# Sparse attention and last block of a three-part transformer kernel: square sums, rotations, constants, selection rounds and norm spreads placed elsewhere

## The reference, cut to what matters

```python
q, k, v, qi, ki, wi = split(h @ w_in)
q = partial_rope(rms_norm(q per head, q_g)); k = partial_rope(rms_norm(k per head, k_g))
score = sum over index heads of wi * relu(qi @ ki.T), -inf above the diagonal
idx = top_k(score, 64)                      # per query
p = softmax(q @ k[idx].T * scale); out = (p @ v[idx]) @ w_o
```

## Time and profile before

| | us |
|---|---|
| median of 3 runs | 1600.78 |
| lowest, highest | 1599.29, 1606.47 |
| the profiled execution's own time | 1597.11 |
| its span (first to last instruction) | 1595.3 |
| TensorE products busy | 1546.4 (97%) |
| VectorE, ScalarE, GpSimd busy | 660.8, 781.2, 1137.6 |
| mean granted TensorE clock | 0.988 |

### The profile page before, as it was taken

How to read it: one execution, slowest core, us unless ns; L and a number is a source line. 1 busy time by engine, 2 the same in 40 slices (tenths; PEclk the granted TensorE clock), 3 DMA queues, 4 the chain that set the end, 5 groups by cost and what they waited for, 6 DMA issues and landing times.

```text
span 1595.3 us, 40789 instructions
## 1 busy us (share of the span) xinstructions
PE 1546.4 (97%) x16162; PEld 1481.1 (93%) x16162; DVE 660.8 (41%) x1615; ACT 781.2 (49%) x1296; POOL 1137.6 (71%) x848
## 2 busy tenths in 40 slices
PE   6999999989999999999999999999999999999998
PEld 6999999878899999999999987699999987799998
DVE  4334468764446333223332257643351435442200
ACT  5444557633345444454444444654445535565532
POOL 5876757983438878778787784088878974478885
PEclk9999999999899999999999999999999999999999
DMA  7544543310023544455444541065536542235552
GB/s 268 185 166 145 178 149 133 106 68 3 2 82 110 198 168 151 164 194 195 167 150 164 188 164 51 10 241 199 183 130 204 192 139 107 80 133 184 185 185 79
DMA packets 37909, 231.31 MB, mean 145 GB/s; under 512 B 4527, under 2 KB 6680, under 8 KB 16552
## 3 DMA queue, kind: packets, MB, share of 16 engines
q1 hardware_dynamic: 36552, 228.57, 40.7%
q10 hardware_dynamic: 1248, 1.24, 0.2%
HBM read 228.67 MB, written 2.63 MB: 145 GB/s over the span
## 4 chain that ended last, share of the span: by engine, by line
PE 74%; DVE 2%; issue 1%; ACT 1%; POOL 0%; DVEq 0%; POOLq 0%; ACTq 0%
PE PS L841 59%; PE PS L840 1%; PE PS L1100 1%; PE PS L1107 1%; PE PS L1515 1%; PE PS L1115 1%; PE PS L1491 1%; PE PS L1139 1%; PE PS L1145 1%; PE PS L1501 1%; PE PS L1291 0%; PE PS L1090 0%; PE PS L1283 0%; PE PS L1679 0%; PE PS L1667 0%
## 5 line engine op out<-in xcount | busy, mean ns | idle before, releaser
L795 POOL TENSOR_TENSOR wlo<-raw,whi 128x256 fp32r<-128x256 f32 (+1 forms) x742 | 1071.1, 1476 | 362.2 <-ACT whi L2739 340.3
L841 PE MATMUL PS<-xh,whi 128*128 128x272 f32 (+1 forms) x2304 | 666.6, 289 | 21.6 <-POOL wlo L795 16.9
L841 PE MATMUL PS<-xl,whi 128*128 128x272 f32 (+1 forms) x2304 | 658.4, 286 | 0.0
L841 PE MATMUL PS<-xh,wlo 128*128 128x272 f32 (+1 forms) x2304 | 657.8, 285 | 0.0
L2739 ACT ACTIVATE whi<-raw 128x1024 fp32r<-128x1024 f32 x468 | 455.4, 982 | 359.3 <-PE PS L841 338.2
L841 PEld LDWEIGHTS PS<-xh,whi 128*128 128x128 f32 x2304 | 434.4, 189 | 31.1 <-issue 23.2
L841 PEld LDWEIGHTS PS<-xl,whi 128*128 128x128 f32 x2304 | 435.6, 189 | 0.5
L841 PEld LDWEIGHTS PS<-xh,wlo 128*128 128x128 f32 x2304 | 436.0, 189 | 0.0
L841 PE MATMUL PS<-hid_h,whi 128*128 128x272 f32 (+1 forms) x960 | 273.8, 285 | 2.1 <-POOL wlo L795 1.6
L841 PE MATMUL PS<-hid_h,wlo 128*128 128x272 f32 (+1 forms) x960 | 273.8, 285 | 0.0
L841 PE MATMUL PS<-hid_l,whi 128*128 128x272 f32 (+1 forms) x960 | 272.8, 284 | 0.0
(11 more groups left out here) (426 smaller groups left out, 1640.3 us busy)
## 6 DMA issues: line engine op xcount, KB each, us to landing
raw<-w_f_in_in SPq DMA_DIRECT2D x88, 1024.0 KB, 4.8
raw<-w_f_dn_in SPq DMA_DIRECT2D x64, 704.0 KB, 4.0
raw<-w_b_ff_in SPq DMA_DIRECT2D x32, 1024.0 KB, 4.8
raw<-w_rk_k_in SPq DMA_DIRECT2D x4, 1024.0 KB, 4.8
raw<-w_rk_r_in SPq DMA_DIRECT2D x4, 1024.0 KB, 4.8
raw<-w_rk_v_in SPq DMA_DIRECT2D x4, 1024.0 KB, 5.1
raw<-w_rk_o_in SPq DMA_DIRECT2D x4, 1024.0 KB, 5.3
raw<-w_at_q_in SPq DMA_DIRECT2D x4, 1024.0 KB, 4.9
```

The costliest lines, as they stand in the source:

```text
L795: last = nc.gpsimd.tensor_tensor(wlo[U % SPL][:, piece], raw[U % RAW][:, piece], whi[U % SPL][:, piece].bitcast(F32), ALU.subtract)
L841: mm(out, a, b, start=start and n == 0, stop=stop and n == 2, **kw)
```

## The change

In the sparse attention TensorE takes the four square sums as 0 and 1 before value tile 0, 2 and 3 before value tile 2. Rotations 1 and 2 are both issued in loop step 0, rotation 3 stays in step 4. The constants go from three groups of six (steps 3, 5, 6) to two groups of three (steps 3 and 5), with the wait of step 6 moved to step 7. On VectorE the last pair of rounds and the end of block 0's selection come before `query_cosine(2)` instead of behind it. In the last block the four pairs of spreads of part a stand two and two: two before and two in the middle of the second half of `b_values(0, .)`; the two key spreads come behind `attend(0)` and `attend(1)`, and VectorE's two key scalings at the end of its steps 1 and 2. The tile of normalised probabilities `prnb` leaves the place where it covered part of the spread table and now covers four tiles of the key's work, for which `krot` is put beside the other three. No instruction on ScalarE, GpSimd or SyncE changes.

```diff
--- before.py
+++ after.py
@@ -447,12 +447,13 @@
         craw = b2("craw", [128, 2, 2, SEQ])
         squares = Region(rings)("squares", [128, 8, SEQ])
         b2.here = rings + 4 * 8 * SEQ
+        prnb = Region(b2.here)("prnb", [128, 2, 2, SEQ])
         kr = b2("kr", [128, SEQ])
         kg = b2("kg", [128, SEQ])
         krs = b2("krs", [32, SEQ])
+        krot = b2("krot", [128, SEQ])
         lgb = Region(b2.here)("lgb", [128, 2, 2, SEQ])
         ksq = b2("ksq", [128, 4, SEQ])
-        krot = b2("krot", [128, SEQ])
         qn = b2("qn", [128, 4, SEQ])
         qr = b2("qr", [128, 2, SEQ])
         qg = b2("qg", [128, 2, SEQ])
@@ -485,8 +486,6 @@
         posf = tb("posf", [128, SEQ])
         freq = tb("freq", [128, 2])
         spread = tb("spread", [16, 1280])
-
-        prnb = Region(posi_at)("prnb", [128, 2, 2, SEQ])
         ptb = tb("ptb", [128, 2, 2, SEQ])
         assert used[0] <= nc.sbuf_usable_end, (used[0], nc.sbuf_usable_end)
 
@@ -1469,15 +1468,15 @@
             last.then_inc(s_hrot, 1)
             query_rotation(0)
             query_sum(0)
+            query_sum(1)
             U, G = U0["at_v"], G0["at_v"]
             pe.wait_ge(s_lo, 2 * U + 2)
             pe.wait_ge(s_free, G - 1)
             pe.wait_ge(s_hsq, 4)
             value_tile(0, PS[:, bank(G), 0:256])
-            query_sum(1)
             query_sum(2)
+            query_sum(3)
             value_tile(2, PS[:, bank(G), 256:512]).then_inc(s_part, 1)
-            query_sum(3)
 
             o0 = G0["at_o"]
             def head_scores(j):
@@ -1537,13 +1536,19 @@
                     head_transposes(j - 1)
                 if 0 <= j - 2 < 16:
                     head_values(j - 2)
-                if j in (1, 2, 4):
-                    if j == 4:
-                        pe.wait_ge(s_hout, 3)
-                    query_rotation({1: 1, 2: 2, 4: 3}[j])
-                if j in (3, 5, 6):
-                    pe.wait_ge(s_hout, {3: 3, 5: 4, 6: 5}[j])
-                    constants(6, PS[:, ahead + (j == 5), 0:128])
+                if j == 0:
+                    query_rotation(1)
+                    query_rotation(2)
+                if j == 3:
+                    pe.wait_ge(s_hout, 3)
+                    constants(3, PS[:, ahead, 0:128])
+                if j == 4:
+                    query_rotation(3)
+                if j == 5:
+                    pe.wait_ge(s_hout, 4)
+                    constants(3, PS[:, ahead + 1, 0:128])
+                if j == 7:
+                    pe.wait_ge(s_hout, 5)
                 if j in (7, 8):
                     output_part(0, j - 7)
                 if j in range(9, 18, 2):
@@ -1580,19 +1585,20 @@
                     if norm and mi == 0:
                         norm_sum(norm, SEQ)
 
-            def b_values(u, q):
+            def b_values(u, q, part=range(4)):
                 name = ("b_va", "b_vb")[u]
                 U, G = U0[name], G0[name]
                 pe.wait_ge(s_lo, 2 * U + q + 1)
                 if q == 0:
                     pe.wait_ge(s_free, G - 1)
-                for k in range(4 * q, 4 * q + 4):
+                for k in [4 * q + d for d in part]:
                     for j in range(2):
                         tb_ = slice(j * 128, j * 128 + 128)
                         last = products(PS[:, G % 2, j * 256:j * 256 + 256], weights(U, ALLR, slice(k * 256, k * 256 + 256)),
                                         (xh[0][:, k, tb_], xl[0][:, k, tb_]), k == 0 and j == 0, k == KC - 1, tokens=True,
                                         skip_group_check=True)
-                last.then_inc(s_unit, 1)
+                if 3 in part:
+                    last.then_inc(s_unit, 1)
 
             def b_queries(u, q):
                 U, G = U0["b_uq"] + u, G0["b_uq"] + u
@@ -1756,29 +1762,42 @@
             pe.wait_ge(s_hinv, AT2 + 1)
             pe.wait_ge(s_rcd, 2)
             pe.wait_ge(b_cc, 1)
-            for n, j in enumerate((0, 4, 2, 6)):
+            def head_spread(n):
+                j = (0, 4, 2, 6)[n]
                 for q in range(2):
                     last = mm(PS[:, 4 + n, q * SEQ:q * SEQ + SEQ], spread_two(16, j + q), hinva[:, :], start=True, stop=True)
                 last.then_inc(s_hb, 1)
-            b_values(0, 1)
-            pe.wait_ge(s_hinv, AT2 + 2)
-            for q in range(2):
-                last = mm(PS[:, 2, q * SEQ:q * SEQ + SEQ], spread_rope(q), hinvb[:, :], start=True, stop=True)
-            last.then_inc(s_hb, 1)
-            for n in range(2):
+
+            def rope_spread():
+                pe.wait_ge(s_hinv, AT2 + 2)
+                for q in range(2):
+                    last = mm(PS[:, 2, q * SEQ:q * SEQ + SEQ], spread_rope(q), hinvb[:, :], start=True, stop=True)
+                last.then_inc(s_hb, 1)
+
+            def key_spread(n):
                 if n:
                     pe.wait_ge(s_hsc, AT_HSC + 5)
                 for q in range(2):
                     last = mm(PS[:, 3 - n, q * SEQ:q * SEQ + SEQ], spread_two(8, 2 * n + q), hinvb[:, :], start=True, stop=True)
                 last.then_inc(s_hb, 1)
+
+            head_spread(0)
+            head_spread(1)
+            b_values(0, 1, range(2))
+            head_spread(2)
+            head_spread(3)
+            b_values(0, 1, range(2, 4))
+            rope_spread()
             pe.wait_ge(s_hsc, AT_HSC + 2)
             scores(0)
             pe.wait_ge(s_x, X0["cq"] + 3)
             b_queries(0, 0)
             attend(0)
+            key_spread(0)
             b_queries(0, 1)
             pe.wait_ge(s_hsc, AT_HSC + 4)
             attend(1)
+            key_spread(1)
             b_queries(1, 0)
             attend(2)
             b_queries(1, 1)
@@ -2419,9 +2438,9 @@
             top_rounds(0, 1)
             dve.wait_ge(s_hroot, 1)
             v.reciprocal(hinvk[0:4, :], hinvk[0:4, :]).then_inc(s_hinv, 1)
-            query_cosine(2)
             top_rounds(0, 1)
             top_end(0)
+            query_cosine(2)
             dve.wait_ge(s_hb, 1)
             dve.wait_ge(s_free, G0["at_k"] + 1)
             v.scalar_tensor_tensor(kT[:, :, :], kT[:, :, :], col(VEC["k_g"]), PS[:, 6:8, 0:T],
@@ -2616,7 +2635,8 @@
             dve.wait_ge(b_rotd, 1)
             v.tensor_tensor(krf[:, :, :], krot[:, :].unsqueeze(1).broadcast_to([128, 2, SEQ]), spread_pair(2),
                             ALU.mult).then_inc(s_hsc, 1)
-            for n in range(2):
+
+            def key_scale(n):
                 dve.wait_ge(s_hb, AT_HB + 6 + n)
                 x = kn[:, 2 * n:2 * n + 2, :]
                 v.scalar_tensor_tensor(x, x, gqk[:, 0:1], spread_pair(3 - n), ALU.mult, ALU.mult).then_inc(s_hsc, 1)
@@ -2686,6 +2706,8 @@
                     dve.wait_ge(s_unit, 2 * (U0["b_uq"] + 1))
                     v.tensor_scalar(qg[:, :, :], chunk_pair(G), col(VEC["qb_r"]), None, ALU.mult).then_inc(b_qg, 1)
                     queries_drain(0, qr[:, :, :])
+                if J in (1, 2):
+                    key_scale(J - 1)
                 if J == 3:
                     queries_drain(1, qn[:, 0:2, :])
                 if J == 4:
```

## The result

| | before | after |
|---|---|---|
| median of 20 runs, us | 1601.45 | 1597.95 |
| lowest, highest | 1597.60, 1612.94 | 1589.15, 1603.93 |
| profiled execution's own time, its span | 1597.11, 1595.3 | 1599.32, 1597.5 |
| its mean granted clock | 0.988 | 0.983 |

The ratio after to before is 0.9972, with a 95% interval of 0.9959 to 0.9984: 4.5 us less (2.6 to 6.6), inside the 0.5% that I call the same. The ratio is estimated over all runs of both; the two medians alone lie 3.5 us apart. The profiled execution of after is 2.2 us slower than that of before although the medians stand the other way. So the two traces can't be subtracted as wholes; they have to be read stage by stage, with the clock beside each length.

What follows compares the result with a forecast made beforehand. TensorE, with 74% of the chain, was taken as the bound. Attention -5.92 us (idle, low clock and constants won, less 3.17 of new waits) and last block +0.2 made -5.7: 1600.78 to 1595.1 us, range 1590.5 to 1599.8.

Steps and rivals of the forecast that it cites:

- (1): Sparse attention, before score products 2: TensorE waits for VectorE's logits 1, 0.53 us.
- (2): Sparse attention, before transposes 0: TensorE waits for VectorE's probabilities 0, 0.71 us.
- (3): Sparse attention, before transposes 1: TensorE waits for ScalarE's copy of transposes 0, behind half a weight copy, 0.87 us.
- (4): Sparse attention, before transposes 2: TensorE waits for ScalarE's copy 1, behind the second half weight copy, 0.76 us.
- (5): Sparse attention, before transposes 3: TensorE waits some 0.30 us, with VectorE's rotation sums 1 and 2 in its steps 2 and 3.
- With the clock full: Sparse attention, steps 0 to 6: filling the hole keeps full clock, winning about 3 us of low clock.
- Rival A: Sparse attention, thinned steps: the clock falls again for 6.8 us, 2.2 us lost, gain 3.5, 1597.3 us; chance 0.17.
- A gain is excluded, since no wait stands there to be filled: Last block, reordered spreads: no time can be won, as TensorE's only waits there lie at 1352 and later.
- the price of changing kinds: Last block: one more change from full products to spreads and back costs 0.2 us, bounds 0 and 0.4.
- B: Sparse attention: ScalarE's and VectorE's strings close up, no new waits, 9.1 us less there, 1591.9 us; chance 0.09.
- D: Sparse attention, steps 1 to 5: VectorE is the bound and the constants were cover, gain 2.6, 1598.2 us; chance 0.10.
- C: Sparse attention: the constants held the clock; without them low clock persists, 1606.6 us with the last block; chance 0.04.

Runs made afterwards that it cites:

- again: The changed kernel unaltered, measured a second time against the kernel before: median 1595.83 us, ratio 0.9958.
- attention_only: The change's attention edits alone, with the last block of the kernel before: 1600.89 us, ratio 0.9997 to the kernel before.
- sums_apart: The changed kernel with the last block's query sums in two halves around half a value tile: 1595.38 us, ratio 0.9955 to the kernel before.
- before_again: The kernel before, unaltered, measured and profiled a second time: 1602.56 us, ratio 0.9999.
- last_block_only: The change's last-block edits alone, with the attention of the kernel before: 1599.47 us, ratio 0.9985 to the kernel before.
- spreads_twice: The kernel before with each of the last block's four pairs of head spreads issued twice: 1609.88 us, ratio 1.0040.
- constants_only: The kernel before with two groups of three constants instead of three of six, rotations unmoved: 1601.08 us, ratio 0.9983.
- no_constants: The changed kernel without any constants in the attention loop: 1598.62 us, ratio 0.9964 to the kernel before.
- fill: The changed kernel with 1 and 3 constants ahead of the transposes of steps 1 and 2, none in steps 3 and 5: 1599.27 us, ratio 0.9973.
- old_constants: The changed kernel with the three groups of six constants put back: 1599.68 us, ratio 0.9974 to the kernel before.
- rotations_only: The kernel before with only rotations 1 and 2 moved into step 0, constants as before: ratio 1.0000.

## Why the prediction was right, and where it was not

Sign, size and class hold: -5.7 forecast, -4.5 (-2.6 to -6.6) measured, and -6.7 by the ratio of the second measurement of the same kernel; the median, 1597.95, lies in the range (1590.5 to 1599.8). Its composition doesn't hold, and that the size came out is in part luck: the low clock that the attention part was to save is hardly saved, and a gain in the last block, which I had excluded, stands in its place.

*Right, the attention at full clock.* The sum gave 20.31; again took 20.62. Of the waits, (1) 0.53 was 0.78, (2) 0.71 was 0.29, (3) 0.87 was 0.93, (4) and (5) together 1.06 were 1.05 for probabilities (994.23 in again), where I had put most of it on ScalarE's copy. In (2) transposes 0 began 1.17 behind score products 2, as forecast (1.16); but score products 2, behind a wait, hold TensorE for 0.87 by their row, not for the 0.45 estimated, 0.42 more. With 0.11 less of waits that makes the 0.31 by which the sum fell short. The 3.08 of constants measured 3.0. The lead through VectorE's string was 0.49 for 0.42. Selection rounds and buffers: zero, as said; no wait for either shows in the stage, and score products 8 to 15 stayed at 19.06.

*Wrong, "With the clock full".* This is the first step that failed. I priced the low clock of stage A at 3 us and took all of it as won, since no new wait is over 0.87. The four profiles of the attention part as changed show spells of 0, 0, 3.4 and 10.2 us, with lengths of 20.62, 20.62, 22.17 and 24.03, a mean of 21.9 (after, again, attention_only, sums_apart). The four with all of its old form (before, before_again, last_block_only, spreads_twice) average 25.8. So the stage won 3.9 of 5.9, and 3.0 of that are the constants. Over all 14 profiles it looks no better: behind the hole of 3.07 us the clock fell in all five that have it, for 3.4 to 6.8 us (5.5 in the mean), and with the hole filled it fell in six of nine, for 3.4 to 13.7 us (6.8 in the mean of the nine). Rival A was put down as another case with a chance of 0.17; it is a state that the same kernel is in or not, from one execution to the next. Its price for one was about right: 24.03 against 20.62 is 3.4 for a spell of 10.2, and I had 2.2 for one of 6.8. Over all runs attention_only shows no clock gain at all (+1.3 ± 1.2). After fell with no hole over 0.93 us, between groups separated by short idles, as the Trainium skill ("TensorE: Matmul & The Clock Gate", section "A second HAM failure mode: psum-queue depth-cycling") has it, and against my reading of the earlier trace rows; again and sums_apart, with holes of at most 1.05 us, did not fall.

*Wrong, "A gain is excluded, since no wait stands there to be filled".* This is the second step that failed. I looked for idle time only, in a profile that happened to hold full clock there. The block form of the spreads had a spell among or right behind them in 4 of 5 profiles besides spreads_twice (mean length of stage B 44.2), the single form none in that place in 8. The six of these whose query sums are whole have a mean length of 42.4: 1.8 won, although four of the six fell behind those sums and only two of the five with the block. Over all runs the low-clock share of last_block_only is 4.9 ± 1.4 lower, of which stage B's profiles explain only a part.

The premise of both, that the clock falls "only after holes", was wrong in the very trace that it was read from. At 471.4 us in before the clock fell with TensorE busy throughout, at the end of a row of 48 matmuls with 2 output columns in the first layer:

```profile
467.23 4.24 PE L1260 MATMUL PS<-sel,gn_squares 128*96 128x2 f32 x48
```

```profile
468.00:470.00 2.00, 2.00 (x26) 2.00 (x25) 0.00 (x0) 0.21 (x1) 1.32 (x2) 1.00 0.64 266
470.00:472.00 2.00, 2.00 (x21) 2.00 (x21) 0.20 (x1) 0.24 (x1) 0.00 (x0) 0.84 0.00 0
```

All 14 profiles have a fall between 464.9 and 471.6 us, none of them with idle time in the 7 us before it. The rows that the prediction rests on come from the two stages alone.

*Mis-sized, the price of changing kinds.* Forecast 0.2, bounds 0 and 0.4. At full clock stage B takes 41.39 (last_block_only) against 40.62: 0.77, outside the bounds. I counted one more change from full products to spreads; there are three: the head spreads (two groups of 1.99 in place of one of 3.72) and both key spreads, now apart. The first of them costs 1.99+1.99-3.72=0.26 by their own rows, and the two key spreads 1.13+1.13-2.06=0.20 by theirs; where the rest of the 0.77 lies is open.

*Rivals.* B (the waits don't come): no; they came. D (VectorE the bound, constants as cover): no; constants_only kept 3.0 of 3.08. C (the constants hold the clock): not in its size, since no_constants gains (0.9964). A smaller effect is open: from 18 constants over 6 to none the low-clock share of the changed kernel goes -4.8, -3.1, -0.5, each ± 1.4, so some of what the constants cost may come back. But fill, with 4, stands at -0.9 ± 1.9. constants_only shows none of it (+0.5 ± 1.4).

*Open.* Why the same code falls in one execution and not in the next, and why old_constants and last_block_only lose so little in all; the stages of this change hold only a small part of the 25 us.

## What to carry to other kernels

One profile that shows full clock in a stage is no proof that the stage holds it: take two or three, and read each stage's length with its granted clock beside it. Look for rows of small matmuls (few rows in, or few columns out) that fill the busy column completely, and try full products between them: the split spreads cost 0.77 us of stage B at full clock, and its mean length was still 1.8 us shorter. For the split sums that isn't shown. When a hole is filled with work taken from behind it, count the idle time of the whole stage: here it was 3.07 us before and 3.06 after, until the next producer in line (a weight copy on ScalarE that wasn't due) was moved as well, which left 1.83.

## What was not expected of the hardware

The clock fell without any idle time ahead of it: at the end of 4.24 us of 2-column sums (before, at 471.4), behind 3.72 us of 16-row spreads (before_again, and not in before), within 10.61 us of them (spreads_twice), behind 2.74 us of 8-column sums (after, again, fill, no_constants, before_again, rotations_only; not in the other six profiles that have them whole, and not behind two halves of 1.40 us in two). It fell behind holes of at most 0.93 us in after, and stayed at full speed through windows in which TensorE was busy 0.96 and 0.95 of 2 us in again. With the same instructions in stage A the low clock lasted 0, 0, 3.4 and 10.2 us. The start of score products 1, behind some 974 us of almost the same code, lay between 974.01 and 985.04 us in the 14 profiles. The clock had been low for 10.2 us ahead of the earliest (old_constants) and for 41.0 us ahead of the latest (spreads_twice), which is the larger part of it, though not all: sums_apart began at 984.08 with 34.1 us. The 11 us between them are more than the change is worth and are why single profiled times of this kernel mislead.
